# Deferred norm in six sites: banks handed over by their last read, four units split ahead of joints, a first chunk ahead of splits and a last chunk in three passes

## The reference

```python
def rmsnorm(x, g):
    y = xf * lax.rsqrt(jnp.mean(xf * xf, axis=-1, keepdims=True) + NORM_EPS)
    return (y * g.astype(jnp.float32)).astype(x.dtype)
...
def swiglu(h, w_gate, w_up, w_down):
    return (jax.nn.silu(h @ w_gate) * (h @ w_up)) @ w_down
...
for layer in range(DEPTH):
    g = norm_gains[layer]
    h = rmsnorm(x, g[0])
    x = x + 0.5 * rmsnorm(swiglu(h, w_ffn_gate[layer, 0], w_ffn_up[layer, 0], w_ffn_down[layer, 0]), g[1])
    h = rmsnorm(x, g[2])
    x = x + rmsnorm(token_mixer(h, w_in[layer], w_out[layer], ...), g[3])
    h = rmsnorm(x, g[4])
    x = x + 0.5 * rmsnorm(swiglu(h, w_ffn_gate[layer, 1], ...), g[5])
```

## Time and profile before

| | us |
|---|---|
| median of 3 runs | 1534.99 |
| lowest, highest | 1534.18, 1543.8 |
| the profiled execution | 1544.76 |
| its span, first to last instruction | 1543.0 |

### The profile page before, as it was taken

The page is one execution under the profiler, slowest core; times in us unless marked ns, Lnnn a source line. Parts: engine busy times, 40 slices in busy tenths (PEclk is TensorE's granted clock), DMA queues, the critical chain, the costliest instruction groups (busy, mean ns, idle before and its releaser), DMA issues.

```text
span 1543.0 us, 22041 instructions
## 1 busy us (share of the span) xinstructions
PE 1468.5 (95%) x8081; PEld 1180.5 (77%) x8081; DVE 997.5 (65%) x1623; ACT 714.9 (46%) x1235; POOL 62.5 (4%) x91
## 2 busy tenths in 40 slices
PE   5899999989999899999999999999999999999998
PEld 3678746767845788878887788877888888778887
DVE  1588335254334677777676777676777775867776
ACT  2533146132245444456565444464444756644443
POOL 0200220110101000000010000000000000000000
PEclk9999999999999999999999999999999999999999
DMA  9622165245315556546333556436564653245562
GB/s 304 204 82 82 55 203 197 82 153 165 110 41 182 169 165 216 191 150 169 132 110 126 187 198 200 158 123 224 174 199 148 207 144 136 96 159 196 190 195 77
DMA packets 197428, 242.94 MB, mean 157 GB/s; under 512 B 4304, under 2 KB 178800, under 8 KB 197232
## 3 DMA queue, kind: packets, MB, share of 16 engines
q1 hardware_dynamic: 194272, 229.43, 45.9%
q0 software_dynamic: 2512, 10.49, 2.0%
q10 hardware_dynamic: 576, 2.10, 0.4%
HBM read 240.95 MB, written 1.05 MB: 157 GB/s over the span
## 4 chain that ended last, share of the span: by engine, by line
PE 79%; DVE 9%; ACT 5%; DMA 4%; issue 3%; POOL 0%; SPq 0%; ACTq 0%; DVEq 0%
PE bank L1651 33%; PE bank L2108 17%; PE bank L2109 8%; PE bank L1740 5%; DVE weights_low L1305 3%; DMA weight_ring<-in_w_ffn_gate 2%; PE bank L2015 2%; ACT weights_high L841 2%; DMA weight_ring<-in_w_ada 2%; PE bank L1629 1%; PE bank L1960 1%; DVE input_split L1336 1%; PE bank L2060 1%; PE bank L1923 1%; PE bank L1882 1%
## 5 line engine op out<-in xcount | busy, mean ns | idle before, releaser
L2108 PE MATMUL bank<-input_split,weights_high 128*128 128x512 f32 x1408 | 502.1, 399 | 2.0 <-DVE input_split L1336 1.7
L1305 DVE TENSOR_TENSOR weights_low<-weight_ring,weights_high 128x1024 fp32r<-128x1024 f32 x328 | 397.9, 1225 | 115.7 <-ACT weights_high L841 114.8
L841 ACT ACTIVATE weights_high<-weight_ring 128x1024 fp32r<-128x1024 f32 x328 | 339.4, 1052 | 200.8 <-PE bank L2109 66.4
L2109 PE MATMUL bank<-input_split,weights_low 128*128 128x256 f32 x1408 | 395.1, 281 | 0.0
L2108 PEld LDWEIGHTS bank<-input_split,weights_high 128*128 128x128 f32 x1408 | 264.6, 188 | 69.0 <-issue 2.5
L2109 PEld LDWEIGHTS bank<-input_split,weights_low 128*128 128x128 f32 x1408 | 266.0, 189 | 3.0
L1651 PE MATMUL bank<-weights_high,hidden_high 128*128 128x512 f32 x352 | 141.5, 402 | 17.3 <-DVE hidden_low L1389 17.3
L1651 PE MATMUL bank<-weights_low,hidden_high 128*128 128x512 f32 x352 | 140.5, 399 | 0.0
L1651 PE MATMUL bank<-weights_high,hidden_low 128*128 128x512 f32 x352 | 139.4, 396 | 0.0
L918 ACT ACTIVATE hidden_high<-hidden 128x256 fp32r<-128x256 f32 x88 | 36.7, 417 | 176.1 <-DVE hidden L1385 172.3
L1651 PE MATMUL bank<-input_split,weights_high 128*128 128x256 f32 x512 | 94.6, 286 | 1.0 <-DVE input_split L1336 0.8
(11 more groups left out here) (318 smaller groups left out, 2080.5 us busy)
## 6 DMA issues: line engine op xcount, KB each, us to landing
weight_ring<-in_w_ffn_gate SPq DMA_DIRECT2D x44, 1024.0 KB, 5.6
weight_ring<-in_w_ffn_up SPq DMA_DIRECT2D x44, 1024.0 KB, 5.3
weight_ring<-in_w_ffn_down SPq DMA_DIRECT2D x44, 1024.0 KB, 5.0
weight_ring<-in_w_in SPq DMA_DIRECT2D x32, 1024.0 KB, 5.4
weight_ring<-in_w_ada SPq DMA_DIRECT2D x24, 1024.0 KB, 6.7
weight_ring<-in_w_out SPq DMA_DIRECT2D x16, 1024.0 KB, 4.9
weight_ring<-in_w_in SPq DMA_DIRECT2D x24, 512.0 KB, 5.1
gain_row<-in_norm_gains POOLq DMA_DIRECT2D x6, 512.0 KB, 4.0
```

The lines of the kernel that those rows point to most:

```text
L841: A(unit_in(WH, U), unit_source(U), ACT.Copy).then_inc(s_high, 1)
L1305: TTn(unit_in(WL, U), unit_source(U), unit_in(WH, U).bitcast(F32), ALU.subtract).then_inc(s_low, 1)
L2108: mm(b[:, :].rearrange("p (h n) -> p h n", h=2), unit_in(WH, U)[:, k, :], HX[:, k, :, :], start=(k == 0), stop=False, skip_group_check=True)
L2109: last = mm(b[:, 0:T], unit_in(WL, U)[:, k, :], HH[:, k, :], start=False, stop=(k == KD - 1), skip_group_check=True)
```

## The change

1. `EARLY` is 4 instead of 3, and the split of the fourth unit leaves `site_norm`. The mixer's tail splits `EARLY` units too.
2. `WARM` is 6 instead of 12.
3. The output banks are handed over by `y_gained` instead of `x_new`, in both kinds of site.
4. ACT takes only the squares (`x_square`) and no small Identity ops between them; the mean is made by DVE in `inverse(i)`, with the reciprocal and the diagonal. In a feed-forward `inverse` stands behind the first reduce; both reduces of the first chunk and one low stand ahead of the wait for `norm_row`, and the low of unit 5 goes behind `hidden_low(0)`.
5. In the feed-forward's last pair, chunk `par` 1 is made by `feature_major` (three passes of 256 columns in one half of a bank). DVE multiplies straight from the bank, without a reduce. The counters `s_added` and `s_up` are then one less in each feed-forward, which `ready - n` takes into account.
6. In the mixer DVE's evictions and lows are written out one by one instead of by `projected`: the two evictions of a pair of units stand together, and of the two lows ahead of a softmax one goes behind it. `lambda_sums` goes ahead of `inverse`, `lambdas` ahead of the first softmax.

The diff, cut to its core:

```diff
-EARLY = 3
-WARM = 12
+EARLY = 4
+WARM = 6
...
+            def x_square(i, t, hf):
+                act.wait_ge(*(at("x_new", i - 1, t, hf) if i else at("final_scaled", t, hf)))
+                A(XN2[:, t, hf * 512:(hf + 1) * 512], X[:, t, hf * 512:(hf + 1) * 512], ACT.Square, accum_out=stat[:, 2 * t + hf:2 * t + hf + 1]).then_inc(*done("sum_squares", "site", i, t, hf))
...
-                high(unit_base[i] + 3)
-                x_mean(i, 1)
-                for t in range(2):
-                    act.wait_ge(*at("x_mean", i, t))
+                for hf in range(2):
+                    x_square(i, 1, hf)
+                act.wait_ge(*at("x_mean", "ready", i))
                 A(stat[:, 8:10], stat[:, 6:8], ACT.Sqrt).then_inc(*done("rms_ready", "site", i))
+                high(unit_base[i] + 4)
...
-                high(unit_base[i] + 5)
+                if SITES[i][0] == "mix":
+                    high(unit_base[i] + 5)
...
                 silu(0, f0 + 1, f0 if n else None)
                 hidden_high(0, f0 + 1, None)
+                high(a + 5)
...
+            def inverse(i):
+                for t in range(2):
+                    for hf in range(2):
+                        dve.wait_ge(*at("sum_squares", "site", i, t, hf))
+                TTn(stat[:, 6:8], stat[:, 0:4:2], stat[:, 1:4:2], ALU.add).then_inc(*done("x_mean", "sum", i))
+                dve.wait_ge(*at("x_mean", "sum", i))
+                TS(stat[:, 6:8], stat[:, 6:8], 1.0 / D, eps[:, 0:1], ALU.mult, ALU.add).then_inc(*done("x_mean", "ready", i))
...
                 a = unit_base[i]
+                gate_parts(0, a + 1)
+                inverse(i)
+                up_parts(0, a + 2)
+                low(a + 4)
                 dve.wait_ge(*at("norm_row", i))
-                gate_sum(0, a + 1, f0 + 1)
-                product(0, a + 2, f0 + 1)
+                gate_scaled(0, f0 + 1)
+                multiplied(0, f0 + 1)
                 hidden_low(0, f0 + 1)
+                low(a + 5)
...
-                gate_sum(1, a + 3, f + 2)
+                dve.wait_ge(s_used, a + 3)
+                TTn(gsum[:, 1, :], B[2][:, 0:T], norm_row, ALU.mult).then_inc(s_gate, 1)
                 low(a + 6)
-                product(1, a + 4, f + 2)
+                dve.wait_ge(s_used, a + 4)
+                dve.wait_ge(s_silu, f + 2)
+                TTn(hbuf[:, 1, :], B[3][:, 0:T], sgate[:, 1, :], ALU.mult).then_inc(s_h, 1)
...
-                projected(10, 12)
+                low(u0 + 15)
+                evicted(11)
+                low(u0 + 16)
                 pair(4)
                 head_out(2)
-                projected(12, 14)
+                low(u0 + 17)
+                evicted(12)
+                evicted(13)
+                low(u0 + 18)
                 pair(5)
...
-                        for r in hand_over(4 + 2 * t + hf, ("x_new", i, t, hf)):
+                        for r in hand_over(4 + 2 * t + hf, ("y_gained", i, t, hf)):
...
                 gate_up(0, a, f - 1)
-                gate_up(1, a + 2, f)
+                pe.wait_ge(s_h, f)
+                for q in range(2):
+                    pe.wait_ge(s_low, a + 3 + q)
+                    feature_major(B[2 + q][:, 0:T], a + 2 + q).then_inc(s_used, 1)
```

117 lines of the change are left out of this document (70 added, 47 removed).

## The result

| | before | after |
|---|---|---|
| executions of the result, median us (number; of the six before, three are those that the forecast had) | 1543.41 (6) | 1525.62 (6) |
| ratio, 95% interval | | 0.9897 (0.9866 to 0.9927) |
| all executions of this study, median us (number) | 1542.3 (70) | 1525.5 (16) |
| lowest and highest of these | 1534.18, 1550.04 | 1521.85, 1529.77 |
| span of the profiled execution | 1543.0 | 1524.6 |

The change makes the kernel 1.0% faster: 17 us over all executions (17.8 over those of the result), where 20 were forecast. The forecast named 1515 us, and 1525.62 came: 5.6 us outside its own range of 1510 to 1520, and just inside the wide one of 1508 to 1526.

What follows compares the result with a forecast made beforehand. TensorE is busy nearly all the time, so only its waits, mostly for VectorE outputs, can be won. Terms 3.7 + 5.0 + 0.6 + 4.4 + 6.3 = 20.0 us, from 1535.0 to 1515 us; range 1510 to 1520, 8 in 10 1508 to 1526.

Steps and rivals of the forecast that it cites:

- Start of site 0: Before feed-forward 0: halved warm-up lets ACT read the first chunk earlier, less 1.15 us for a late low; 3.7 us gained.
- Joints: Between sites: hand-over by y_gained lets the first tile's transposes run ahead; 1.0 us in each of five, 5.0 us.
- Last chunk and fourth unit: Behind feed-forwards: dropped reduces bring hidden_low earlier, nearly cancelled by one more low; 0.2 us a joint, 0.6 us.
- Heads: Start of four feed-forwards: first hidden_low wait vanishes (1.25 us), a later transfer wait grows 0.15; 1.1 each, 4.4 us.
- Mixers: Two mixers: evictions no longer behind lows, so projection waits shrink, less a new wait for unit 4; 6.3 us gained.
- rival 3: Cold start at site 0: lowered clock cuts that gain to about 1.7 us, joints lose 1 us each; 1522 us, chance 0.08.
- Transfers decide the heads: Feed-forward heads: the load behind the second wait keeps its time, so 4.4 us are waited off; 1519.4 us, chance 0.12.
- Mixer order and joints don't help: New lows replace old mixer waits, DVE's queue binds joints; only start, heads and half the joints stay; 1524.4 us, chance 0.13.
- Slower by three passes: Feed-forwards' last chunk: each pass takes 0.28 us, costing 3.8 us in each of 8 units; 1545.4 us, chance 0.03.
- Nothing happens: Whole kernel: the waits only change names; 1533 to 1536 us, chance 0.04.
- `hidden_low` releases PE 5 times and not 7: Sign in PE's waits: forecast 7 releases by hidden_low instead of 11, four at about 3 us, three at about 0.4 us.
- Wrong if the waits of 2.3 to 3.0 us grew by the full 1.25 us: Sign against the forecast: feed-forwards' second wait, for a transfer, taking back all the head gain; forecast growth was 0.15 us.

Runs made afterwards that it cites:

- experiment 8: Units 6 and 7 split earlier in the feed-forward heads, so loads issue earlier: 1509.67 us in the changed kernel, 1530.0 us alone in the kernel before.
- experiments 4 and 6: Changed kernel with banks handed over by x_new again, 1525.45 us (hand-over by y_gained alone in the kernel before, 1536.89); changed kernel with old mixer order, 1526.54 us.

## Why the prediction was right and where it was wrong

**The sum held,** in part by luck: 20.0 us forecast, 19.9 by stages, 19.3 by time × clock, but joints and mixers gave 1.7 us less than forecast and the last chunk and the heads 1.7 more. Term by term:

- *Start of site 0*: 3.7 against 3.65, shown by undoing it. The late low part costs its 1.15 us, as reckoned.
- *Joints*: 5.0 against 4.4; undone 4.95. Ahead of a feed-forward a joint gained its 1.0 us, ahead of a mixer only 0.7: there the residual of the second tile still makes PE wait 0.31 us, since PE, freed earlier by the shorter last chunk, is ahead of DVE with its fourth unit (with the wide last chunk there is no such wait, and these joints take 3.47 us, not 3.73). The forecast had this as the cost of the fourth unit and put it into the next term.
- *Last chunk and fourth unit*: 0.6 against 1.5 (2.03 less 0.55 on the way there). The 0.82 us wait went in two of the three sites and fell to 0.52 in the third, and the restart with it; I had let the wait shrink by 0.5. The three passes cost 0.008 us a k, less than the earlier trace rows can show.
- *Heads*: 4.4 against 5.2 between the two first profiles; two more executions of the changed kernel gave 5.7 and 8.3, so the term is known to some 3 us. The first wait went, 1.29 us, and 0.26 us at `norm_sum` that I had not seen. Its cause was named wrongly by more than half: 1.0 of the 1.55 us doesn't need the new order of the head, and neither do 1.0 of the 1.3 us by which the loads go out earlier.
- *Mixers*: 6.3 against 5.2. The waits for the projections are gone as foreseen, but PE kept 5.2 of the 6.6 us. The new wait for unit 4 is 0.35 us in both mixers, where 0.55 and 0.1 were forecast.

**The step that failed** is "from the median of the runs, which lies 9.8 us below the profiled one without a visible reason in the stages touched, 1535.0 − 20.0 = **1515 us**". The words "without a visible reason" were the warning. Three executions that stood at 1534.18, 1534.99 and 1543.8, and a fourth, the profiled one, at 1544.76, have two of four near 1544; the median of three fell on the low pair. The step took that low base as if the profile's extra 9.8 us could be left out, and no run ever showed it again: 67 later executions of the kernel before never came below 1537.8, and 64 of them have a mean of 1542.2, 7.2 us above the 1535.0. The forecast's other sum, 1544.8 − 20.0 = 1524.8, had the profile's own terms and the profile's own base, and the profiled execution after took 1526.42 us: 1.6 off, which is the first block's 1.54. Of the 10.6 us by which 1515 missed, some 7 are this base, 2 the clock, and the rest is within what executions differ by. Why the first two were low is open, as said.

**The clock** was looked for at the wrong place. The granted clock is 1.00 from 484 to 490 us and in all five joints (682 to 687 and so on), so rival 3 didn't come. It acts where the forecast let a wait stand. The waits at the third down product of 3.35, 3.43, 2.44 and 2.50 us were each followed by PE at half clock: the way to the fourth one took 9.98 to 10.07 us, instead of the 8.48 to 8.50 of experiment 8, so 1.5 to 1.6 us were lost each time in this execution. I had reckoned the waits themselves and their growth, but what follows them not at all; it was there before as well (0.72 from 528 to 532 us; 10.07 to 10.10 us), and waits and clock together were a larger thing to win than any term of the sum: 14.4 us in experiment 8. The Trainium skill ("TensorE: Matmul & The Clock Gate", A second HAM failure mode: psum-queue depth-cycling) says of another kernel that short idle times between groups of matmuls made the clock go down and up, and that throughput was lost to slowing down and warming up again. The traces here agree that each time costs, 1.5 to 1.6 us.

**The rivals.** *Transfers decide the heads* (1519.4): the waits grew by 0.39 and 1.09 us in sites 0 and 2 and not in the others (-0.18, 0.02) between the two first profiles, and experiment 8 moved the landing by the order of the splits: refuted as a cap, though what is left of the wait is a transfer's. *Mixer order and joints don't help* named 1524.4, nearly the measured time, and is refuted by experiments 4 and 6: the number fitted by chance. *Slower by three passes*: 0.12 us a site instead of 7.6. *Nothing happens*: refuted.

**What was to be seen.** `hidden_low` releases PE 5 times and not 7, since the waits in the tails of sites 0 and 3 are gone altogether; the waits of 1.04 and 1.35 us are gone; eight transposes stand behind the last wait of a joint ahead of a mixer, not four, and none ahead of a feed-forward. "Wrong if the waits of 2.3 to 3.0 us grew by the full 1.25 us": one of four nearly did (1.09), in this execution; in another of the changed kernel the same wait was 2.45 us, 0.11 more than before.

## What to carry to other kernels

Take the terms and the base of a forecast from the same execution, and where the shown runs and the profile disagree by half of what you forecast, let the range cover both instead of choosing the lower. Look at what makes a load's issue wait, not only at what makes a product wait: two splits that stood behind work that they had nothing to do with cost 14 us in four places. Where the parts of a change are smaller than the spread of the executions, read each from its stage of the trace; medians of four executions put two real terms of near 5 us (experiments 4 and 6) at 0.0 and 1.1.

## What the runs showed of the hardware that I had not expected

- How much is lost to the clock behind one and the same wait differs between executions of one kernel. In three profiled executions of the changed kernel the way from down 3 to down 4 of a feed-forward took 8.5 us (at full clock), 10.0 to 10.1, or 11.3 (nearly twice as much lost).
- The length of PE's wait alone doesn't decide it: a wait of 3.03 us was followed by 8.48 us, one of 1.79 us by 10.08, in the same execution.
- The spread of the first block, 10.8 us over 16 profiled executions, goes in part with such stretches: it ended first where 10.2 us were lost to the clock up to 470 us, and last where 20.5 were. But of two executions with the same 15.4 us lost, one reached that point at 473.59 and the other at 478.83, so something else differs too, and no run shows what.
- A load of 1 MB took 5.3 to 5.6 us from issue to landing when the load ahead of it had been issued 3.7 us before, and 7.0 to 8.0 when that was 1.5 us before (the third gate slot, in experiment 8 and in the first profiles of both kernels). The exception is site 0 of the changed kernel with the earlier splits, with 7.0.
